# Two transformer blocks on one core: separate slots for the modulation weights, attention heads four units apart, and turns moved in the mixer

## The reference, cut to what matters

```python
mod = (c @ w_mod[l] + b_mod[l]).reshape(B, N_MOD, D)      # 2048 -> 6 x 2048
shift_m, scale_m, gate_m = mod[:, 0, None], mod[:, 1, None], mod[:, 2, None]
shift_f, scale_f, gate_f = mod[:, 3, None], mod[:, 4, None], mod[:, 5, None]
h = rms_norm(x, g_pre_mix[l]) * (1 + scale_m) + shift_m
proj = h @ w_in[l]
y_a = gmlp_spatial_gating(proj[..., COL_UV:COL_QLAT], ...)
y_b = dsa_attention(q, k, v, q_idx, k_idx, idx_w)         # 8 heads, top-64 keys by an index score
gates = jax.nn.sigmoid(proj[..., COL_GATE:])
merged = gates[..., :D] * (y_a @ w_proj_a[l]) + gates[..., D:] * (y_b @ w_proj_b[l])
mix_out = merged @ w_out[l]
x = x + gate_m * rms_norm(mix_out, g_post_mix[l])
h2 = rms_norm(x, g_pre_ffn[l]) * (1 + scale_f) + shift_f   # then the FFN with gate_f, then block two
```

## Time and profile before

| | us |
|---|---|
| median of 3 runs | 2596.39 (2596.05 to 2600.30) |
| the profiled execution | 2599.43 |
| its span, first to last instruction | 2597.7 |
| PE busy | 2456.1 (95%) |
| VectorE busy | 1626.6 (63%) |
| ScalarE busy | 1132.7 (44%) |
| mean granted TensorE clock | 0.984 |

### The profile page before, as it was taken

How to read it: one execution, slowest core, us unless ns; L and a number is a source line. 1 busy time by engine, 2 the same in 40 slices (tenths; PEclk the granted TensorE clock), 3 DMA queues, 4 the chain that set the end, 5 groups by cost and what they waited for, 6 DMA issues and landing times.

```text
span 2597.7 us, 33272 instructions
## 1 busy us (share of the span) xinstructions
PE 2456.1 (95%) x11340; PEld 2032.6 (78%) x11340; DVE 1626.6 (63%) x2022; ACT 1132.7 (44%) x1442; POOL 1.9 (0%) x7
## 2 busy tenths in 40 slices
PE   4989999988897999999999998999999999999998
PEld 3667777766676888888888887888778899999887
DVE  6788887867766666444444445455555567777554
ACT  3434444543345444443444335444543454544443
POOL 0000000000000000000000000000000000000000
PEclk8999999999998999999999999999999999999999
DMA  8887558886784877555555554665465554445554
GB/s 284 294 282 269 187 194 272 279 283 220 259 272 136 273 264 256 174 192 186 183 173 188 189 189 158 198 198 199 157 198 182 174 164 158 151 152 171 176 181 138
DMA packets 152587, 535.97 MB, mean 206 GB/s; under 512 B 17200, under 2 KB 18480, under 8 KB 152240
## 3 DMA queue, kind: packets, MB, share of 16 engines
q1 hardware_dynamic: 150480, 527.24, 61.3%
q10 hardware_dynamic: 2016, 7.47, 0.8%
HBM read 532.55 MB, written 2.10 MB: 206 GB/s over the span
## 4 chain that ended last, share of the span: by engine, by line
PE 75%; DMA 9%; DVE 9%; ACT 4%; issue 3%; DVEq 0%; SPq 0%; ACTq 0%
PE acc L1436 23%; PE acc L1437 23%; PE acc L1438 23%; DMA raw<-in_wa_dram 9%; DVE lo L820 4%; ACT hi L436 2%; PE tb L1489 1%; PE tb L1849 1%; DVE macc L847 1%; DVE macc L965 0%; PE tb L1852 0%; PE tb L1839 0%; PE tb L1438 0%; PE tb L1436 0%; PE tb L1437 0%
## 5 line engine op out<-in xcount | busy, mean ns | idle before, releaser
L820 DVE TENSOR_TENSOR lo<-raw,hi 128x1024 fp32r<-128x1024 f32 (+3 forms) x844 | 980.9, 1172 | 775.6 <-ACT hi L436 773.3
L436 ACT ACTIVATE hi<-raw 128x1024 fp32r<-128x1024 f32 (+3 forms) x844 | 850.2, 1018 | 1072.2 <-PE acc L1438 682.8
L1436 PE MATMUL acc<-hi,Hh 128*128 128x512 f32 x1984 | 802.5, 404 | 21.2 <-DVE lo L820 10.0
L1437 PE MATMUL acc<-lo,Hh 128*128 128x512 f32 x1984 | 788.7, 398 | 0.0
L1438 PE MATMUL acc<-hi,Hl 128*128 128x512 f32 x1984 | 788.3, 397 | 0.0
L1436 PEld LDWEIGHTS acc<-hi,Hh 128*128 128x128 f32 x1984 | 376.3, 190 | 122.8 <-DVE lo L820 9.4
L1438 PEld LDWEIGHTS acc<-hi,Hl 128*128 128x128 f32 x1984 | 375.5, 189 | 91.0
L1437 PEld LDWEIGHTS acc<-lo,Hh 128*128 128x128 f32 x1984 | 375.8, 189 | 87.1 <-issue 1.4
L1436 PE MATMUL acc<-hi,hbh 128*128 128x384 f32 (+1 forms) x640 | 228.3, 357 | 0.0
L1438 PE MATMUL acc<-hi,hbl 128*128 128x384 f32 (+1 forms) x640 | 222.8, 348 | 0.0
L1437 PE MATMUL acc<-lo,hbh 128*128 128x384 f32 (+1 forms) x640 | 222.7, 348 | 0.0
(11 more groups left out here) (258 smaller groups left out, 1890.9 us busy)
## 6 DMA issues: line engine op xcount, KB each, us to landing
raw<-in_wa_dram SPq DMA_DIRECT2D x840, 512.0 KB, 4.4
raw<-in_wb_dram SPq DMA_DIRECT2D x128, 384.0 KB, 3.4
raw<-in_wc_dram SPq DMA_DIRECT2D x64, 512.0 KB, 3.4
x<-in_x_dram ACTq DMA_DIRECT2D x2, 2048.0 KB, 9.2
out_dram<-x SPq DMA_DIRECT2D x8, 256.0 KB, 2.8
poolM<-in_pool_dram ACTq DMA_DIRECT2D x1, 768.0 KB, 4.3
raw<-in_wa_dram SPq DMA_DIRECT2D x4, 160.0 KB, 3.7
wsT<-in_ws_dram ACTq DMA_DIRECT2D x1, 512.0 KB, 4.1
```

The costliest lines, as they stand in the source:

```text
L436: act.activation(hi[:, s, 0:n], raw[:, r, 0:n], ACT.Copy).then_inc(hi_ready, 1)
L820: dve.tensor_tensor(lo[:, s, 0:n], raw[:, r, 0:n], hi[:, s, 0:n].bitcast(F32), ALU.subtract)\
L1436: pe.matmul(dst(tt), a, hi[:, s, w], start=first and i == 0, stop=False)
L1437: pe.matmul(dst(tt), a, lo[:, s, w], start=False, stop=False)
```

## The change

- The modulation units of the start and of the quarters get six slots `start_raw`, the late ones up to the out stage get four slots `late_raw`, in memory that is free then. SP issues them in the same queue, at the same place in the order of units, but each waits for its own slot (`mod_used`). The last 32, in the FFN, stay in the ring of `raw`.
- `LATE` has 44 late units in the gates, one per unit from `GATES0 + 20`, 30 in the merge and 22 in the out stage; none in the fourth quarter.
- In the start, the scaling of `x` by its root goes from VectorE to ScalarE, and VectorE asks for the root after modulation unit 4 and not 8. In quarters two to four ScalarE writes the scaled input over `xnT` and rounds it with one more copy, and VectorE no longer computes its own version.
- Heads stand 4 units apart from `GATES0 + 23`, not 5 from `GATES0 + 24`. ScalarE copies `pt1` at H+7, not H+8. `output` comes after unit H+5, not H+4. The spatial product comes three units later, `index_keys` one unit.
- Six of the eight turns of `y` stand between the last units of the gates and two after the merge's first two units; before, all were at the gates' end or in the merge. The merged tile is turned after the third unit of the next tile and not the second, with two `tok` buffers.
- The rows of `gate_m` are spread in the out stage, one group of 512 after each of units 3 to 6; before, all four stood together in the merge. The second load of `x` is issued in the out stage and not at the start of the merge.

```diff
--- before.py
+++ after.py
...
-SPATIAL0 = GATES0 + 12
-HEAD_AT = [GATES0 + 24 + 5 * head for head in range(HEADS1)]
...
+SPATIAL0 = GATES0 + 15
+HEAD_AT = [GATES0 + 23 + 4 * head for head in range(HEADS1)]
...
+TURN0 = GATES0 + 57
...
-LATE = (spaced(K3B, 20, 6) + spaced(GATES0 + 14, 10, 6) + spaced(GATES0 + 24, 40, 40) + spaced(MERGE0, 32, 28) +
-        spaced(OUT0, 20, 16) + spaced(FFN0 + 8, 64, 32))
+LATE = spaced(GATES0 + 20, 44, 44) + spaced(MERGE0, 32, 30) + spaced(OUT0, 24, 22) + spaced(FFN0 + 8, 64, 32)
...
+START_SLOTS, LATE_SLOTS = 6, 4
+RING_LATE = (LATE_WIDE - 2) * KD
...
+        start_raw = [sb(f"start_raw{i}", [P, UNIT], at=at) for i, at in enumerate(
+            (q_at, q_at + 4 * KB, free + 24 * KB, free + 28 * KB, free, free + 4 * KB))]
+        late_raw = [sb(f"late_raw{i}", [P, UNIT], at=at) for i, at in enumerate(
+            (q_at, q_at + 4 * KB, x_at, x_at + 8 * KB))]
...
+            def load_start(m):
+
+                if m >= START_SLOTS:
+                    sp.wait_ge(mod_used, m - START_SLOTS + 1)
+                sp.dma_start(start_raw[m % START_SLOTS][:], wa[m]).then_inc(start_loaded[m % START_SLOTS], 16)
+
...
+                if i == 0:
+                    sp.wait_ge(unit_used, RING + Q3B + 2)
+                if i == 2:
+                    sp.wait_ge(gmlp_ready, 4)
+                if i >= LATE_SLOTS:
+                    sp.wait_ge(mod_used, START_UNITS + i - LATE_SLOTS + 1)
+                sp.dma_start(late_raw[i % LATE_SLOTS][:], wa[START_UNITS + i]).then_inc(late_loaded[i % LATE_SLOTS], 16)
...
+            for m in range(KD):
+                load_start(m)
+            for unit in range(FFN0):
+                if unit in START_AT:
+                    q, kt = START_AT[unit]
+                    load_start(q * KD + kt)
+                if unit in LATE:
+                    load_late(LATE.index(unit))
+                load(wa[RING_MODS + unit][:, 0:4 * 80 if unit in NARROW else UNIT])
...
-                    ins = act.activation(Hh[:, k, :], xnT[:, k, :], ACT.Identity, scale=fA[:, k:k + 1],
-                                         bias=modfm[:, shift:shift + 1])
+                    ins = act.activation(Hh[:, k, :] if q == 0 else xnT[:, k, :], xnT[:, k, :], ACT.Identity,
+                                         scale=fA[:, k:k + 1], bias=modfm[:, shift:shift + 1])
+                if q > 0:
+                    ins.then_inc(in_scaled, 1)
+                    act.wait_ge(in_scaled, q)
+                    ins = act.activation(Hh[:, 4 * q:4 * q + 4, :], xnT[:, 4 * q:4 * q + 4, :], ACT.Copy)
...
+            act.wait_ge(rstd_ready, 1)
+            for tt in range(TT):
+                act.activation(xn[:, tt, :], x[:, tt, :], ACT.Copy, scale=rstd[:, tt:tt + 1]).then_inc(xn_ready, 1)
...
-                exp_of, since_exp = divmod(upto - HEAD_AT[0] - 5, 5)
-                turn_of, since_turn = divmod(upto - HEAD_AT[0] - 8, 5)
+                exp_of, since_exp = divmod(upto - HEAD_AT[0] - 5, 4)
+                turn_of, since_turn = divmod(upto - HEAD_AT[0] - 7, 4)
...
+                if 0 <= upto - TURN0 - 4 < 6:
+                    act.wait_ge(tr_split, c.up("split"))
+                    take_hi(Hh, 2 * (upto - TURN0 - 4), (upto - TURN0) % 2)
...
-            take_hi_tile(Hh, 0)
-            take_hi_tile(Hh, 4)
-
...
-            spread_rows(gm1)
-
...
-            take_hi_tile(mergedh, 0)
...
+            for j in range(4):
+                split_to(MERGE0 + 8 * j + 14)
                 take_hi_tile(mergedh, j * 4)
...
+            for q in range(4):
+                split_to(OUT0 + 7 + q)
+                act.wait_ge(row_ready, c.up("row"))
+                act.activation(gm1[:, q * N:(q + 1) * N], tb[:, 2, :], ACT.Copy).then_inc(tb_free[2], 1)
...
+                if t == 1:
+                    split_to(OUT0 + 25)
+
+                    act.wait_ge(mod_used, START_UNITS + RING_LATE)
+                    act.dma_start(x[:], x_in).then_inc(x_loaded, 16)
...
+                if kt == 4:
                     dve.wait_ge(ssq_ready, c.up("ssq"))
                     rms(D)
-                    for tt in range(TT):
-                        dve.tensor_scalar(xn[:, tt, :], x[:, tt, :], rstd[:, tt:tt + 1], None, ALU.mult).then_inc(xn_ready, 1)
...
-            for head in range(HEADS1):
-                split_to(HEAD_AT[head] + 5)
-                dve.wait_ge(s_ready, c.up("s"))
-                masked_scores(att1, [(att1[:, keys[tt]], tb[:, 0, keys[tt]], selb[:, keys[tt]], tb_free[0] if tt else None)
-                                     for tt in range(TT)], [(tt, keys[tt]) for tt in range(TT)])
-                split_to(HEAD_AT[head] + 9)
-                dve.wait_ge(exp_ready, c.up("exp"))
...
+            for head in range(HEADS1 + 1):
+                if head < HEADS1:
+                    split_to(HEAD_AT[head] + 5)
+
+                    dve.wait_ge(tr_copy, COPIES_BEFORE_K2 - HEADS1 + head)
+                    dve.wait_ge(s_ready, c.up("s"))
+                    masked_scores(att1, [(att1[:, keys[tt]], tb[:, 0, keys[tt]], selb[:, keys[tt]], tb_free[0] if tt else None)
+                                         for tt in range(TT)], [(tt, keys[tt]) for tt in range(TT)])
+                if head > 0:
+                    split_to(HEAD_AT[head - 1] + 10)
+                    attended(head - 1)
+                if head < HEADS1:
+                    split_to(HEAD_AT[head] + 8)
+                    dve.wait_ge(exp_ready, c.up("exp"))
+                    chain(dve.reciprocal(resum[:], esum[:]))
...
+            def merge_a(j):
+                split_to(MERGE0 + 8 * j + 7)
+                tile_done(3)
...
+                    dve.tensor_tensor(tok[:, j % 2, tt, :], acc[:, tt, :], sg[:, tt, cols(j * N, N)], ALU.mult)\
+                        .then_inc(acc_free[tt], 1)
...
+            def merge_b(j):
+                split_to(MERGE0 + 8 * j + 11)
+                tile_done(3)
...
+                    dve.wait_ge(acc_free[2 + tt], j + (TILES_BEFORE_MERGE // 2 + 2))
+                    ins = dve.tensor_tensor(tok[:, j % 2, tt, :], tok[:, j % 2, tt, :], sgt[:, tt, :], ALU.add)
+                ins.then_inc(tok_ready, 1)
+                split_to(MERGE0 + 8 * j + 14)
+                take_lo_tile(mergedl, mergedh, j * 4)
...
-                tile_done()
...
-                for tt in range(TT):
...
-                ins.then_inc(tok_ready, 1)
-                take_lo_tile(mergedl, mergedh, j * 4)
...
             part_tile(q3, 0, after={1: index_weights})
...
-            part_tile(q3, 1, after={0: index_keys})
-            tile(qlath, qlatl, 0, 2, after={0: lambda: turned(0)})
+            part_tile(q3, 1)
+            tile(qlath, qlatl, 0, 2, after={0: index_keys, 1: lambda: turned(0)})
...
-                head, step = divmod(u - HEAD_AT[0], 5)
-                if 0 <= head < HEADS1:
-                    if step == 0:
-                        scores(head)
-                    if step == 3:
-                        key_major(head)
-                    if step == 4:
-                        output(head)
+                head, step = divmod(u - HEAD_AT[0], 4)
+                if step == 1 and 1 <= head <= HEADS1:
+                    output(head - 1)
+                if step == 0 and 0 <= head < HEADS1:
+                    scores(head)
+                if step == 3 and 0 <= head < HEADS1:
+                    key_major(head)
...
+            def turn_y(k):
+
+                if k < 4:
+                    src = lambda tt, j: z[:, tt, GW + (2 * k + j) * P:GW + (2 * k + j + 1) * P]
+                else:
+                    if k % 2 == 0:
+                        taken(2)
+                    src = lambda tt, j: O1[:, tt, (2 * k - 8 + j) * P:(2 * k - 7 + j) * P]
+                transpose_pair(src, k % 2, tr_split)
+                split_y.append((tb_free[k % 2], c.at(f"tb{k % 2}") + 1))
...
+            def spread_gate_m(q):
                 pe.wait_ge(gate_ready, 1)
-                spread(lambda j: fG[:, j:j + 1], lambda q: 2)
-
-            def second_attended():
-                attended(1)
-                spread_gate_m()
+                fill(2)
+                for j in range(4):
+                    ins = pe.matmul(tb[:, 2, j * P:(j + 1) * P], fG[:, 4 * q + j:4 * q + j + 1].to_broadcast([P, P]), ident[:],
+                                    start=True, stop=True)
+                ins.then_inc(row_ready, 1)
...
-            tile(Hh, Hl, 0, 4, before=split_y, after={1: lambda: attended(0), 3: second_attended})
-            tile(Hh, Hl, 1, 4, k=8, before={0: split_now})
+            tile(Hh, Hl, 0, 4, before=when_split(split_y[0:4]), after={0: lambda: turn_y(6), 1: lambda: turn_y(7)})
+            tile(Hh, Hl, 1, 4, k=8, before=when_split(split_y[4:8]))
             for j in range(1, 4):
-                hooks = {1: lambda: turned(0, tr_split)}
-                tile(Hh, Hl, 0, 4, after=hooks)
+                tile(Hh, Hl, 0, 4, after={2: lambda: turned((j - 1) % 2, tr_split)})
```

(19 more changed lines are left out.)

167 lines of the change are left out of this document (74 added, 93 removed).

## The result

The changed kernel takes 2500.86 us (median of 4 runs, 2499.94 to 2501.2), the kernel before 2598.35 us (4 runs in the same sitting, 2596.05 to 2601.58): 0.9623 of it, 95% interval 0.9607 to 0.964. It is 97.5 us faster; 72.7 were forecast. The sign and the stages of the gain were right.

A forecast was written before the change was run, and what follows sets the result against it. The ring's turn bounds the quarters; TensorE plus its stalls bounds the gates. Gains 5.0 + 16.6 + 2.6 + 16.4 + 30.5 + 1.6 = 72.7 us, from span 2597.7 to 2525.0, forecast 2524 us; range 2506 to 2560.

The forecast's parts named there:

- Which stages gain: Gains by stage: start 5.0, quarters 16.6, fourth quarter 2.6, gates 16.4, merge 30.5, out 1.6 us; later stages nothing.
- The start: Start, 47.4 us: `x` scaled on ScalarE, six slots, last modulation unit starting at about 31.5 us; gain 5.0 us.
- The reserves: Time allowed above TensorE's floors: quarters 57.5 us each against 53.7, gates 214.4 against 205.4, merge 102.6 against 95.6.
- The floors: TensorE's time with waits and half clock gone: 53.7 us a quarter, 205.4 in the gates, 95.6 in the merge.
- upper bounds: Largest gain thought possible per stage: quarters 27, gates 25, merge 37 us; where all stages' upper bounds meet, 2492 us.
- The reason in gates and merge: Gates and merge: TensorE's waits for `pt` and `tok` go by moving steps in the order; gains 16.4 and 30.5 us.
- The key turn: Fourth quarter: `index_keys` a unit later and six modulation units fewer, 89.1 to 86.5 us, gain 2.6 us.
- First rival: Quarters and merge: DMA engines stay at the quarters' old rate, 300 GB/s, a quarter 60 us, 2540 us; chance 0.17.
- Second rival: Gates and merge: VectorE becomes the bound with heads four units apart, TensorE waits for the exponential, 2545 us; chance 0.13.
- Given back in the out stage: Out stage: its 54 loads take 101 us at 300 GB/s, 5 us less gain, 2529 us; inside the forecast's range.
- SP's queue: Quarters and late units: a late load waiting for its slot holds the weight behind it; slower, 2607 us; chance 0.04.

The follow-up runs named there:

- all in the ring: Changed kernel with every modulation unit back in the ring of `raw`, the new order of units kept: 2581.4 us.
- the start's slots alone: Changed kernel with only the late modulation units back in the ring of `raw`, six slots kept for start and quarters: 2546.1 us.
- The added VectorE work: Changed kernel with one more VectorE operation (128 x 384 elements, results unused) with each late unit from the ninth on: 2505.2 us.

## Why the prediction was wrong, point by point

- **Which stages gain: right.** The ring's turn set the pace of the quarters; with the modulation units out of it they fell to TensorE's time (195.0 us with all in the ring, 161.4 with the start's slots alone). `ScalarE <- DMA` in the quarters went from 109.8 us in 50 waits to 14.1 in 8. FFN and FFN-down stayed within 0.2 us, the out stage came 1.3 us under its forecast.
- **The start: right,** gain 5.9 for 5.0. The last modulation unit starts at 31.26 us, 31.5 were forecast; the last eleven stand back to back on VectorE (14.49 us), so that VectorE sets the pace there. The hit is in part luck: they follow each other at 1.32 us and not at the 1.20 that the sum took from the quarters, and 1.1 us of waiting for loads is left between them and not 2. With all in the ring the start is 44.4 us, so half of the gain is the orders'.
- **The reserves: this is the step that failed.** The floors, 53.7 us a quarter, 205.4 for the gates, 95.6 for the merge, were all right: measured 53.2, 55.4, 53.5; 204.4; 96.3. To them I added 3.8 a quarter, 9 and 7, because "all three are close to one another" and VectorE "keeps its lead only narrowly", 27 us in all. Measured, these are 1.0, -1.0 and 0.7 over the floors: together 0.7 us. So 26.7 us of the reserves were not needed, and the profiled gain, 99.7 us, is 27.0 over the 72.7 forecast (start, fourth quarter and out took 0.9 less, 1.9 more and 1.3 less than forecast). The added VectorE work shows that VectorE at 94% of TensorE's time cost it nothing in the gates, where the loads landed ahead. One reserve had a named event, SP holding the third late load until the spatial product is done. The event came, SP waited 11.9 us there, and it cost TensorE nothing. The prediction's own upper bounds were 27, 25 and 37 us for quarters, gates and merge; measured were 27.0, 26.4 and 36.8. Its range left out the low end, where these bounds meet. That the floors came out is no proof of their reasons: they take every wait and all of the half clock off, whatever removes them.
- **The reason in gates and merge: wrong.** The prediction had the waits for `pt` and `tok` go by order. With slots and the old order of `pt` nothing comes back, with slots and the merge's old order 3.2 us. With all in the ring and the new orders, 21.2 us come back in the gates and 19.7 in the merge. There the rows for `pt` and `tok` are gone, so the orders did what was said of them, but the time goes to waits for `att` and `lo`. The slots did it in the gates, and more than half of it in the merge: ScalarE and VectorE work in order, and a `hi` that waits for its load holds the copy behind it. I read "TensorE waits for `pt`" as a matter of where `pt` stands, and never asked in the same stage what ScalarE itself was waiting for, which was 78.1 us of loads.
- **The key turn: wrong sign.** I counted "`index_keys` a unit later" among the reasons of a gain of 2.6. The new place of the two turns costs 4.5 us of the stage: at the old one it gains 5.2. ScalarE's copy was left ahead of a `hi`, which accounts for 1.2 of the gap of 3.3 us.
- **First rival (DMA no faster than in the quarters): fell.** 340 and 324 GB/s in the first two quarters and 338 in the merge, against 291, 281 and 252 in the earlier trace rows. The shares are 0.90, 0.89 and 0.93 there, so the DMA engines were not the limit before.
- **Second rival (VectorE bound by the heads): fell** in the gates, where VectorE is busy 183.4 of 204.4 us. Its sign, TensorE waiting for the exponential, shows only with the late units in the ring (9.4 us with all of them there). In the merge it stands at 93.1 of 96.3 and would be next.
- **Given back in the out stage: fell.** It has 302 GB/s and no wait of TensorE.
- **SP's queue: fell with six and four slots** and with four and three; real with two.

The sum of the profiles' gains is 5.9 + 27.0 + 0.7 + 26.4 + 36.8 + 2.9 = 99.7 us, against 98.9 in the spans (2597.7 to 2498.8).

## What to carry to other kernels

When an engine on the path waits for another, look up in the same stage what that other one waits for in its own order. Two streams that share a ring delay each other through in-order engines; slots of their own were worth about 80 us here (78 with four and three of them), and the moved consumers with the rest of the change about 20 in the ring. With the slots in place, of the two orders tried one gave 3.2 us of its stage and the other nothing; the table, the scaling on ScalarE, the turns of `y` and the rows of `gate_m` were not undone one by one. And where the loads land ahead, forecast a stage at the largest busy sum of its engines: in this kernel a second sum at 94 to 97% of it needed no reserve. A step that is moved later must take along whatever waits for it on the other engines.
